# Sample rows first in scatter, adds and norms, and three smaller moves around them, in a two-layer streaming trunk

## The reference, cut to what matters

```python
def rmsnorm(x, g):
    y = xf * lax.rsqrt(jnp.mean(xf * xf, axis=-1, keepdims=True) + RMS_EPS)
    return (y * g)
# layer 0: h @ w_in -> mLSTM heads and retention heads -> @ w_out      (gates: log_sigmoid)
# layer 1: h @ w_in -> causal convolution over 4 rows, gated DeltaNet -> @ w_out
#          beta = sigmoid(bt);  g = -exp(a_log) * softplus(at + dt_bias)
# after each: x = x + hier_moe(rmsnorm(x, norm_ffn[layer]))
# at the end: y = rmsnorm(x, norm_final)
```

## Time and profile before

| | |
|---|---|
| runs of the kernel | 1498.42, 1501.09, 1501.21 us; median 1501.09 |
| profiled execution | 1499.96 us, of which the span is 1498.1 us |
| mean granted clock of TensorE | 0.969 of 2.4 GHz |
| TensorE busy | 1304.8 us (87%) |
| VectorE, ScalarE, GpSimd busy | 465.3, 247.8, 64.2 us |
| DMA | 453.99 MB, mean 303 GB/s |

### The profile page before, as it was taken

The page is one execution under the profiler, slowest core; times in us unless marked ns, Lnnn a source line. Parts: engine busy times, 40 slices in busy tenths (PEclk is TensorE's granted clock), DMA queues, the critical chain, the costliest instruction groups (busy, mean ns, idle before and its releaser), DMA issues.

```text
span 1498.1 us, 35378 instructions
## 1 busy us (share of the span) xinstructions
PE 1304.8 (87%) x15666; PEld 843.1 (56%) x15666; DVE 465.3 (31%) x1211; ACT 247.8 (17%) x635; POOL 64.2 (4%) x100
## 2 busy tenths in 40 slices
PE   8999889999887887987799978989999888798795
PEld 6645546555554554554478656556566455465453
DVE  1023445432122221221333745344223222122132
ACT  2123213110100100000322422223001010000011
POOL 2000103000000000000200101010000000000000
PEclk9999799999999999999899997999999999999998
DMA  9743135999999999999733300138999999999996
GB/s 284 162 91 120 64 119 222 365 400 427 428 429 428 430 428 428 428 429 423 211 113 113 115 4 15 52 147 338 398 401 427 429 428 428 427 430 429 429 427 255
DMA packets 53002, 453.99 MB, mean 303 GB/s; under 512 B 5553, under 2 KB 6097, under 8 KB 28353
## 3 DMA queue, kind: packets, MB, share of 16 engines
q1 hardware_dynamic: 51024, 448.35, 74.2%
q0 software_dynamic: 1904, 4.58, 1.1%
HBM read 449.55 MB, written 3.35 MB: 302 GB/s over the span
## 4 chain that ended last, share of the span: by engine, by line
PE 71%; DMA 19%; DVE 6%; issue 3%; ACT 1%; POOL 0%; DVEq 0%; SPq 0%; ACTq 0%; POOLq 0%
PE bank L326 68%; DMA W<-in_moe_w_up 18%; PE bank L329 3%; DVE zT L2257 1%; DVE zT L2252 1%; DMA conv_sb<-in_conv_state 1%; DVE zT L2262 1%; DVE HN L1510 0%; DMA X<-in_x_prompt 0%; DVE X L1510 0%; DVE TM L1510 0%; DVE gain L1510 0%; DVE W L1530 0%; DVE W L1519 0%; DVE W L1514 0%
## 5 line engine op out<-in xcount | busy, mean ns | idle before, releaser
L326 PE MATMUL bank<-W,zT 128*32 128x128 f32 (+2 forms) x10304 | 660.1, 405 | 87.9 <-DMA W<-in_moe_w_gate 32.5
L326 PEld LDWEIGHTS bank<-W,zT 128*32 128x32 f32 (+1 forms) x10304 | 390.4, 125 | 323.9 <-DMA W<-in_moe_w_gate 43.2
L2252 DVE TENSOR_TENSOR zT<-zT,bank 128x128 f32<-128x128 f32 x64 | 18.4, 288 | 464.8 <-PE bank L326 464.8
L326 PE MATMUL bank<-W,HT 128*32 128x128 f32 (+1 forms) x768 | 136.7, 394 | 5.9 <-ACT TM L1231 2.3
L326 PE MATMUL bank<-HT,W 128*128 128x288 f32 x512 | 128.9, 412 | 3.1 <-ACT zT L1224 3.1
L1483 ACT COPY zT<-bank 32x256 f32<-32x256 f32 x128 | 46.7, 364 | 448.6 <-PE bank L326 447.0
L326 PEld LDWEIGHTS bank<-HT,W 128*128 128x128 f32 x512 | 97.3, 192 | 31.0 <-ACT zT L1224 3.8
L326 PE MATMUL bank<-zT,HN 128*128 128x128 f32 (+1 forms) x832 | 101.4, 281 | 1.1 <-DVE HN L1510 0.7
L326 PEld LDWEIGHTS bank<-zT,HN 128*128 128x128 f32 (+1 forms) x832 | 95.8, 192 | 8.8 <-issue 7.4
L2262 DVE COPY zT<-bank 32x256 f32<-32x256 f32 x128 | 53.3, 416 | 137.2 <-PE bank L326 135.2
L326 PEld LDWEIGHTS bank<-W,HT 128*32 128x32 f32 (+1 forms) x768 | 61.6, 141 | 60.0 <-issue 54.0
(11 more groups left out here) (279 smaller groups left out, 882.5 us busy)
## 6 DMA issues: line engine op xcount, KB each, us to landing
W<-in_moe_w_down SPq DMA_DIRECT2D x64, 2048.0 KB, 23.2
W<-in_moe_w_gate SPq DMA_DIRECT2D x62, 2048.0 KB, 21.3
W<-in_moe_w_up SPq DMA_DIRECT2D x62, 2048.0 KB, 22.6
W<-in_ab_w_in SPq DMA_DIRECT2D x8, 2048.0 KB, 16.2
W<-in_c_w_in SPq DMA_DIRECT2D x8, 2048.0 KB, 17.0
W<-in_ab_w_out SPq DMA_DIRECT2D x2, 2048.0 KB, 8.0
TM<-in_moe_w_gate SPq DMA_DIRECT2D x2, 2048.0 KB, 20.0
zT<-in_moe_w_up SPq DMA_DIRECT2D x2, 2048.0 KB, 19.4
```

The source lines that it names most:

```text
L326: return nc.tensor.matmul(out, lhsT, rhs, start=start, stop=stop)
L2252: v.tensor_tensor(hid[u % 2], sg[u % 2], banks[u % 2][:, 0:P], ALU.mult).then_inc(m["hidden"], 1)
```

## The change

`TILE_ORDER = (2, 0, 1)` replaces 0, 1, 2 wherever the three tiles are normed from scratch: in TensorE's, ScalarE's, VectorE's and GpSimd's `norm`, in the load of `X`, in the final norm and in the stores. The first constants and the norms' gains are now loaded between tile 2 and tile 0. In `scatter` and `adds` tile 2 comes first, in bank 4; tile 0 and the first half of tile 1 take banks 5, 6, 7, and the second half of tile 1 takes bank 4 after tile 2's adds. ScalarE makes one dummy Square before its first wait for a load. The two loads into `conv_sb` count on a semaphore of their own, `conv_in`, for which only VectorE waits, ahead of the convolution. ScalarE does `projected(0)` before `log_gate`, and `log_gate` calls Ln last.

```diff
+TILE_ORDER = (2, 0, 1)
@@ TensorE
-                small_projection(16, 2, 6, beside=range(1))
+                small_projection(16, 2, 4, beside=range(1))
@@ scatter
-                    for i in range(4):
-                        t, h = i // 2, i % 2
-                        mm(banks[4 + i][:, :], share[0][:, P * t:P * t + P], ys[:, 512 * h:512 * h + 512]
-                           ).then_inc(m["scattered"], 1)
-                    pe.wait_ge(m["added"], SCATTERS * b + SCATTERS + 1)
                     for q in range(4):
                         last = mm(banks[4][32 * q:32 * q + 32, 0:256], share[0][:, 2 * P:N_ALL],
                                   ys[:, 256 * q:256 * q + 256])
                     last.then_inc(m["scattered"], 1)
+                    for i in range(4):
+                        t, h = i // 2, i % 2
+                        if i == 3:
+                            pe.wait_ge(m["added"], SCATTERS * b + SCATTERS + 1)
+                        mm(banks[(5, 6, 7, 4)[i]][:, :], share[0][:, P * t:P * t + P], ys[:, 512 * h:512 * h + 512]
+                           ).then_inc(m["scattered"], 1)
@@ ScalarE
-                act.wait_ge(moe[l]["added"], nb * SCATTERS + (2, 4, 5)[t])
+                act.wait_ge(moe[l]["added"], nb * SCATTERS + (3, 5, 1)[t])
@@ log_gate
                 do(nc.scalar.activation(t24b[:, 0:3 * w], t24a[:, 0:3 * w], ACT.Exp, scale=-1.0))
-                do(nc.scalar.activation(t24b[:, 0:3 * w], t24b[:, 0:3 * w], ACT.Ln, bias=ones[:, 0:1]))
                 if e:
                     do(nc.scalar.activation(t24c[:, :], beta[:, :], ACT.Exp, scale=-1.0))
                     do(nc.scalar.activation(gb1, gb1, ACT.Exp))
+                do(nc.scalar.activation(t24b[:, 0:3 * w], t24b[:, 0:3 * w], ACT.Ln, bias=ones[:, 0:1]))
@@ layer_ab (layer_c alike, with log_gate(8, True))
-                log_gate(4, False)
                 for c in range(8):
                     projected(c, L1, ACT.Copy, float(P) ** -0.5 if c >= 4 else 1.0)
+                    if c == 0:
+                        log_gate(4, False)
@@ ScalarE, start
+            E["blank"].wait(act)
+            do(nc.scalar.activation(junk[:, 0:1], TM[:, 0, 0:1], ACT.Square))
@@ VectorE, norm (ScalarE's norm alike)
-                scaled(0)
-                scaled(1)
-                normalised(0, i)
-                scaled(2)
-                normalised(1, i)
-                normalised(2, i)
+                first, second, third = TILE_ORDER
+                scaled(first)
+                scaled(second)
+                normalised(first, i)
+                scaled(third)
+                normalised(second, i)
+                normalised(third, i)
@@ VectorE, layer_c
-                small_in[2].wait(dve, 96)
+                small_in[2].wait(dve, 64)
...
+                conv_in.wait(dve, 32)
@@ VectorE, adds
-                    for i in range(4):
-                        t, h = i // 2, i % 2
-                        x = X[:, t, 512 * h:512 * h + 512]
-                        dve.wait_ge(m["scattered"], SCATTERS * b + SCATTERS + i + 1)
-                        v.tensor_tensor(x, x, banks[4 + i][:, :], ALU.add).then_inc(m["added"], 1)
-                    dve.wait_ge(m["scattered"], SCATTERS * b + 2 * SCATTERS)
+                    dve.wait_ge(m["scattered"], SCATTERS * b + SCATTERS + 1)
                     for q in range(4):
                         x = X[:32, 2, 256 * q:256 * q + 256]
                         ins = v.tensor_tensor(x, x, banks[4][32 * q:32 * q + 32, 0:256], ALU.add)
                         ins.then_inc(m["added"] if q == 3 else m["quarter"], 1)
+                    for i in range(4):
+                        t, h = i // 2, i % 2
+                        x = X[:, t, 512 * h:512 * h + 512]
+                        dve.wait_ge(m["scattered"], SCATTERS * b + SCATTERS + i + 2)
+                        v.tensor_tensor(x, x, banks[(5, 6, 7, 4)[i]][:, :], ALU.add).then_inc(m["added"], 1)
@@ SyncE, loads of X (stores of y alike)
-            for t in range(TILES):
-                if t == 1:
+            for t in TILE_ORDER:
+                if t == 0:
                     dma(const[:, 0:CONST_HEAD], a["const"][:, 0:CONST_HEAD], const_head_in)
                     dma(gcol[:], a["norm_cols"], gcol_in)
@@ GpSimd
-                    load(cconv[:, :, 0:4], a["conv_taps"], small_in[2])
-                    load(cconv[:, :, 4:7], a["conv_state"], small_in[2])
+                    load(cconv[:, :, 0:4], a["conv_taps"], conv_in)
+                    load(cconv[:, :, 4:7], a["conv_state"], conv_in)
```

More of the change, by code:

```diff
@@ L283, in trunk @@
         small_in = [ev(f"small_in{i}") for i in range(4)]
-        small_used, hgain_in = ev("small_used"), ev("hgain_in")
+        small_used, hgain_in, conv_in = ev("small_used"), ev("hgain_in"), ev("conv_in")
         x_ready, ss_ready, rs_ready = ev("x_ready"), ev("ss_ready"), ev("rs_ready")
@@ L1177, in norm @@
             def norm(x_there):
-                x_there(0)
-                squares(0)
-                x_there(1)
-                squares(1)
-                scaled(0)
-                x_there(2)
-                squares(2)
-                scaled(1)
-                scaled(2)
+                first, second, third = TILE_ORDER
+                x_there(first)
+                squares(first)
+                x_there(second)
+                squares(second)
+                scaled(first)
+                x_there(third)
+                squares(third)
+                scaled(second)
+                scaled(third)
             def take_x(t):
@@ L1326, in layer_c @@
                 norm(lambda t: added(nb, 0, t))
-                log_gate(8, True)
                 for p in range(7):
@@ L1331, in layer_c @@
                             projected(c, L1)
+                            if c == 0:
+                                log_gate(8, True)
                             if p == 5:
```

## The result

| | before | changed |
|---|---|---|
| median of 20 runs each | 1497.80 us (1490.17 to 1501.21) | 1488.62 us (1483.10 to 1500.16) |
| ratio, 95% interval | | 0.9938 (0.9922 to 0.9953) |
| profiled execution, span | 1499.96, 1498.1 us | 1485.65, 1483.8 us |
| mean granted clock in it | 0.969 | 0.974 |

The change won 0.6%, 9.3 us of 1497.8, with an interval of 7.0 to 11.7. Two later sets of runs of the same changed kernel gave 0.9934 (0.9912 to 0.9956) and 0.9937 (0.9913 to 0.9961).

The account below looks back on a forecast made before the run. TensorE paces the mixers and early expert quads, w_up loads the later quads; time won before an expert stage is kept. Terms -1.5 - 3.4 - 1.7 - 0.1 + 0.7 = -6.0 us gave 1494.5 us, range 1490.5 to 1498.5.

Parts of the forecast that it names:

- Layer C's start: Step into layer C: norm and conv loads win 1.5 us, stall before chunk 2 3.4, slow clock in chunk 2 1.7.
- Conv loads and order together: Before layer C's `small_projection`: no wait for conv loads (1.1 us) and tile 2 first (0.35) start TensorE 1.5 us earlier.
- The stall and the clock behind it: Layer C: TensorE's 3.42 us pause before chunk 2 goes, and the 1.7 us lost to 1.2 GHz in chunk 2.
- The norm's own slow stretch before `small_projection` stays: Layer C's norm: TensorE as sparse as before, so no clock gain there; 1.9 us more if the clock stayed up.
- rival 1: Larger gain: clock stays up before layer C's `small_projection`, or first w_in piece comes earlier; about 1492.8 us, chance 0.17.
- The start: Kernel's start: `small_projection` could start 1.5 us earlier, but chunk 0 waits for its weights; gain 0, bounds -1.5 and +0.3.
- The stall for chunk 0's bank in layer 0: Kernel's start, layer 0: a wait of 0.23 us for chunk 0's bank, its removal worth about 0.1 us.
- The scatters: Scatters of the other expert quads: TensorE's time stays 4.24 us, nobody waits for VectorE's earlier end; gain 0.
- The end: Last scatter to span's end: a full tile now comes last and GpSimd's factors are held; 0.7 us lost.
- chunk 3 did not stall: Rival in layer C: chunk 3 waits for `log_gate`, or the clock falls all the same; about 1497 us, chance 0.13.
- nothing in layer C hid the gain: Rival: something later in layer C, independent of TensorE, such as VectorE's convolution, sets its end; 1501 to 1502 us, chance 0.05.
- the fourth wide product did not wait: Rival in all 16 quads' scatters: fourth wide product waits for tile 2's adds; 1504.5 us at 0.6 us each, chance 0.03.

Follow-up runs that it names:

- the kernel with three additions: Changed kernel plus idle products among layer C's norm transposes, final norm and stores ordered 0, 1, 2, second w_in piece of layer 0 held back: 1488.53 us, ratio 0.9921.

## Why the prediction was wrong, point by point

**Layer C's start** was right. Conv loads and order together gave 1.60 us (1.5 forecast), of which the order's share in the norm is 0.46 (0.35), read from the kernel with the old order. The stall and the clock behind it gave 5.07 (5.1). The kernel that undoes only the logarithm's place lost its 2.1, the one that makes only that change won 5.07 in the same stretch, and no later piece gave it back: from there to the experts it took 269.41 us, and 271.64 in the kernel before.

**"The norm's own slow stretch before `small_projection` stays"** is the step that failed. It was put at 0, with up to 1.9 us more only as a bound and as rival 1, and the argument was that TensorE is as sparse there as before. It is not quite: with the new order and 8 products ahead of the norm, five of seven profiles keep 2.4 GHz through `small_projection` and two lose part of it; with the old order all three lose it. The term measures -1.7 us on average, with a standard error of 0.4 (worked out). That the clock there goes with TensorE's activity was shown from both sides, by a profile each: idle products among the transposes keep the clock up with the old order (and with the new one, in the kernel with three additions), and without the 8 products it falls with the new one. That the order alone moves it is likely and not shown: the chance above is one in 12. The prediction had this as rival 1, with 0.17, and its reason there, that the transposes follow the idle products more closely, was the better one.

**The start** was right as a mechanism: the earlier norm went into a longer wait for the piece of weights. The norm gained less than the 1.5 us forecast: 0.9 in the first pair, 0.6 on average (`small_projection` starts at 15.0 over eight profiles of the new order of loads, at 15.6 over four of the old). The stall for chunk 0's bank in layer 0, put at 0.1, gave 0.04: from chunk 0 to `cumulate` 19.99 us before and 19.95 after. Over eight profiles chunk 0 starts between 20.33 and 22.29 us with the new order of loads (mean 20.9), and over four with the old one between 20.99 and 22.46 (mean 21.7). Whether the order of loads wins part of these 0.7 us stays open, the spread being as large.

**The scatters** of the other quads were right: both expert stages are as long as before.

**The end** cost 0.3 us for a forecast of 0.7. The adds ended 5.0 and not 5.55 us after the scatter, because back-to-back adds take 0.63 each and the narrow products are ready sooner.

**The sum** of what repeats is -1.60 - 1.66 - 5.07 + 0.33 = -8.0 us. The runs give somewhat more. Set by set, each against the runs of the kernel before in its own set, the means differ by 9.0 us (20 and 20 runs), 9.7 (26 and 6) and 9.1 (21 and 10), with standard errors of 1.2, 0.9 and 1.7 (all worked out). So about 1 us more than the sum was won; that may be chance, and no piece of the traces shows where it would lie. The forecast of 6.0 was short by 2 us in the pieces, nearly all of it the clock before `small_projection`, and by about 3 in the runs.

**The base** did the rest: 1494.5 was a base of 1500.5 less 6.0. The range was laid around a median of three runs, 1501.09, and one profiled execution of 1499.96, while 20 runs give 1497.80; less 6.0 that is 1491.8, inside the range. The range took the spread of three runs, 2.8 us, for the kernel's, and it is 11 us from the lowest to the highest of 20. Nor do two profiles give the difference: of the 14.3 us between them, 4.8 lie in layer 0's mixer and 2.3 late in layer C. The first follows the slow stretches. The window from 150 to 206 us has a granted clock of 0.79 in the kernel before, and the mixer takes 238.5 us; a changed kernel at 0.79 takes 238.6; those at 0.91 take 232.8, with the old order of tiles as with the new (the kernel with extra products in the mixer apart). So this piece is not the change's doing. The 2.3 us are less clear: the granted clock of this piece is 0.96 in both profiles, with slow stretches at other points of the work. Elsewhere it took 265.1 to 273.3 us, and 270.4 and 269.8 in the two later profiles of the changed kernel. Over the 20 runs of the changed kernel times and mean clocks go together from 1483.1 us at 0.979 to 1500.16 at 0.966 (correlation -0.78). What decides in which executions the clock falls at 178 us stays open.

Of the rivals, the first has the half on the clock in the result; its other half, an earlier first piece of w_in, has not. The others had nothing: chunk 3 did not stall, nothing in layer C hid the gain, and the fourth wide product did not wait (the scatter's 16 products take 4.27 us without a pause, 4.24 before).

## What to carry to other kernels

Cut two traces at common marks before putting their difference down to a change: here half of it lay in pieces that the change does not touch and that move from execution to execution, and the marks gave each part to 0.1 us where the ratios could not. When a change moves work around a stretch in which TensorE is sparse, price the clock of the stretch behind it as a term of its own, with both levels as its cases. And take a base for an absolute forecast from as many runs as there are, for with three the median can stand 3 us off.

## What the runs showed of the hardware

Pauses of TensorE of 2.29 and 2.41 us left the clock at 2.4 GHz, one of 3.57 us was followed by 1.2 GHz, in one profile each. And without 8 idle products of 2 us in all, in a time in which TensorE has nothing else to do, one profile lost 3.4 us behind them, and 12 runs more than that.

A GpSimd operation of 0.19 or 0.56 us that starts while VectorE multiplies two operands from SBUF is held until that ends: 1.25 and 1.05 us for 0.19, 1.43 for 0.56. One that ran beside VectorE's adds, with one operand in PSUM, took 0.18. The Trainium skill ("SBUF — State Buffer", section "Who interferes with whom") states that a VectorE instruction with two SBUF inputs contends with a GpSimd instruction that reads SBUF, because both use one port pair, which it calls an exclusive lock. The traces agree: the first kind ended 0.05 to 0.06 us after VectorE's, the second 0.40 after.
